# A decoder step on one core: QKV order, per-head statistics, paired heads and the division moved to GpSimd

## The reference, cut to what matters

```python
q = rmsnorm(q, q_gain); k = rmsnorm(k, k_gain)      # per head, over 64 dims
scores = einsum(q, k) * 64 ** -0.5                  # query block against own and previous block of 128
scores = where(valid, scores, -inf)                 # 0 <= qpos - kpos < 128
probs = softmax(concat([scores, sink], -1))[..., :-1]
o = einsum(probs, v) @ w_o
```

## Time and profile before

| | us |
|---|---|
| median of 3 runs | 1272.03 |
| the runs | 1272.03, 1272.52, 1254.83 |
| profiled execution, its own time | 1270.31 |
| profiled execution, span | 1268.5 |
| mean granted TensorE clock | 0.948 of 2.4 GHz |

### The profile page before, as it was taken

The page is one execution under the profiler, slowest core; times in us unless marked ns, Lnnn a source line. Parts: engine busy times, 40 slices in busy tenths (PEclk is TensorE's granted clock), DMA queues, the critical chain, the costliest instruction groups (busy, mean ns, idle before and its releaser), DMA issues.

```text
span 1268.5 us, 25324 instructions
## 1 busy us (share of the span) xinstructions
PE 1199.8 (95%) x9702; PEld 1153.2 (91%) x9710; DVE 726.9 (57%) x1164; ACT 450.4 (36%) x748; POOL 394.5 (31%) x833
## 2 busy tenths in 40 slices
PE   5998799899999999999999777999999999999998
PEld 4985566799999999999998777999999999999998
DVE  6653277467777525776533673454767732676731
ACT  5221245344444213444442123233544411444410
POOL 6046666677878767300003264000000000000000
PEclk9996599999999999999996588999999999999999
DMA  7320200123335333222655232222222322322323
GB/s 245 135 79 25 77 26 26 51 91 120 104 123 178 125 105 109 98 96 98 245 147 134 80 101 79 79 87 96 83 86 99 102 92 73 100 83 99 101 92 103
DMA packets 51206, 129.13 MB, mean 102 GB/s; under 512 B 16940, under 2 KB 20268, under 8 KB 51152
## 3 DMA queue, kind: packets, MB, share of 16 engines
q1 hardware_dynamic: 46880, 115.54, 27.9%
q0 software_dynamic: 4272, 12.89, 2.8%
HBM read 109.91 MB, written 18.21 MB: 101 GB/s over the span
## 4 chain that ended last, share of the span: by engine, by line
PE 86%; DVE 7%; ACT 3%; DMA 2%; issue 2%; SPq 0%; ACTq 0%; DVEq 0%
PE ps L1293 25%; PE ps L1295 25%; PE ps L1294 25%; PE ps L1487 2%; ACT probs L692 2%; PE ps L1337 1%; DVE probs L1052 1%; PE ps L1531 1%; PE ps L1492 1%; DMA x<-in_xT 1%; PE ps L1383 1%; DVE soft L1036 1%; PE ps L1539 1%; DMA rots<-e_scr 1%; PE ps L1452 1%
## 5 line engine op out<-in xcount | busy, mean ns | idle before, releaser
L1293 PE MATMUL ps<-hx_hi,w_hi 128*128 128x260 f32 x1600 | 454.3, 284 | 17.7 <-DVE w_lo L842 11.6
L1295 PE MATMUL ps<-hx_hi,w_lo 128*128 128x260 f32 x1600 | 452.6, 283 | 0.0
L1294 PE MATMUL ps<-hx_lo,w_hi 128*128 128x260 f32 x1600 | 451.2, 282 | 0.0
L590 ACT ACTIVATE w_hi<-w_raw 128x1024 fp32r<-128x1024 f32 (+1 forms) x156 | 175.9, 1127 | 494.7 <-PE ps L1295 494.7
L1293 PEld LDWEIGHTS ps<-hx_hi,w_hi 128*128 128x128 f32 x1600 | 301.6, 189 | 20.2 <-DVE w_lo L842 10.9
L1295 PEld LDWEIGHTS ps<-hx_hi,w_lo 128*128 128x128 f32 x1600 | 301.5, 188 | 0.0
L1294 PEld LDWEIGHTS ps<-hx_lo,w_hi 128*128 128x128 f32 x1600 | 301.4, 188 | 0.1
L842 DVE TENSOR_TENSOR w_lo<-w_raw,w_hi 128x1024 fp32r<-128x1024 f32 (+1 forms) x156 | 205.8, 1320 | 102.4 <-ACT w_hi L590 102.3
L1293 PE MATMUL ps<-hid_hi,w_hi 128*128 128x260 f32 x704 | 199.1, 283 | 0.0
L1294 PE MATMUL ps<-hid_lo,w_hi 128*128 128x260 f32 x704 | 198.7, 282 | 0.0
L1295 PE MATMUL ps<-hid_hi,w_lo 128*128 128x260 f32 x704 | 198.7, 282 | 0.0
(11 more groups left out here) (246 smaller groups left out, 1741.3 us busy)
## 6 DMA issues: line engine op xcount, KB each, us to landing
w_raw<-in_wup SPq DMA_DIRECT2D x88, 512.0 KB, 3.2
w_raw<-in_wdn SPq DMA_DIRECT2D x32, 704.0 KB, 4.0
w_raw<-in_wglu SPq DMA_DIRECT2D x16, 512.0 KB, 3.3
w_raw<-in_wqkv SPq DMA_DIRECT2D x12, 512.0 KB, 3.3
w_raw<-in_wo SPq DMA_DIRECT2D x8, 512.0 KB, 3.4
g_scr<-rec POOLq DMA_DIRECT2D x8, 512.0 KB, 3.0
c_scr<-rec POOLq DMA_DIRECT2D x8, 512.0 KB, 3.0
wst<-g_scr SPq DMA_DIRECT2D x8, 512.0 KB, 8.1
```

The source lines that it names most:

```text
L590: act.activation(w_hi[b][:, 0:kt * P], w_raw[b][:, 0:kt * P], ACT.Copy).then_inc(hi_done, 1)
L1293: pe.matmul(out, wh, xh, start=(k == 0), stop=False)
L1294: pe.matmul(out, wh, xl, start=False, stop=False)
L1295: ins = pe.matmul(out, wl, xh, start=False, stop=(k == kt - 1))
```

## The change

Order and statistics: keys and values are projected first (`qkv_tile`, also in SP's load). Squares, statistics and turns stand among the units. `head_mean` is now a 128x128 block matrix written by VectorE. Keys: its product with the squares gives the mean on all partitions, then square root and reciprocal (`key_rstd`), and `key_norm` writes the output keys and `kp`, the prompt's keys with both gains. Prompt queries are not scaled any more: four matmuls of two columns per tile (`query_stat`) give one value per token on the partition, and its negative inverse times the scale (`nq_rms`) enters the new pass over the scores. The parameter work starts at unit 0 instead of 1 and 2.

Heads: scores and values of two heads alternate between the array's halves. One `tensor_tensor_reduce` per block adds the mask, scales and takes the minimum with the sink, from PSUM into one of six `probs` buffers. ScalarE's exponentials go in place. GpSimd multiplies by the inverse sums. ScalarE copies all seven turned blocks of the even head, VectorE those of the odd. Sample parts stand between pairs. The rest of SP's list, `tables` and all later stages are as before.

```diff
+def qkv_tile(n, b):
+    return 2 * n + b + (8 if isinstance(n, int) and n < 2 else -4)
...
@@ gpsimd
             pool.wait_ge(conv_in, 48)
             pre_rows()
+            for a in range(HEADS):
+                pool.wait_ge(sem("r_done"), a + 1)
+                for blk in range(NB):
+                    v = probs[a % 6][:, blk * 256 + lowest(blk):blk * 256 + 256]
+                    ins = pool.tensor_scalar(v, v, soft_of(a)[2][:, blk:blk + 1], None, ALU.mult)
+                ins.then_inc(sem("p_done"), 1)
             pool.wait_ge(sem("bb_done"), 1)
@@ vector
+            def masked(j, half):
+                dve.wait_ge(sem(f"scored{half}"), j + 1)
+                for e in range(2):
+                    a = 2 * j + e
+                    for blk in (2 * half, 2 * half + 1):
...
+                        ins = dve.tensor_tensor_reduce(
+                            probs[a % 6][:, blk * 256 + lo:blk * 256 + 256],
+                            ps[:, 2 * e + half, c0 + lo:c0 + 256], mask[:, lo:256],
+                            nq_rms[:, n:n + 1], nsink[:, h:h + 1], ALU.add, ALU.min,
+                            soft_of(a)[0][:, blk:blk + 1])
+                    if half:
+                        ins.then_inc(sem("maxed"), 1)
+                    elif e == 1:
+                        ins.then_inc(sem("first_taken"), 1)
+
+            def weights(a):
+                dve.wait_ge(sem("exp_done"), a + 1)
+                _, s, r = soft_of(a)
+                after(tt(s, s, r, ALU.add))
+                dve.reciprocal(r, s).then_inc(sem("r_done"), 1)
...
+            for j in range(NPR):
+                if j + 2 < NPR:
+                    masked(j + 2, 0)
+                attn_turn(2 * j + 1)
+                if j + 1 < NPR:
+                    weights(2 * j + 2)
+                if j in (1, 2):
+                    attn_out(j - 1)
+                if j + 2 < NPR:
+                    masked(j + 2, 1)
...
+                if j >= 3:
+                    attn_out(j - 1)
+                if j + 1 < NPR:
+                    weights(2 * j + 3)
@@ scalar
+            for j in range(NPR):
+                attn_turn(2 * j)
+                if j + 1 < NPR:
+                    attn_exp(2 * j + 2)
...
+                if j >= 1:
+                    attn_out(j - 1)
+                if j + 1 < NPR:
+                    attn_exp(2 * j + 3)
@@ tensor
+            for u in range(12):
+                unit("qkv", u // 2, u % 2, hx_hi, hx_lo, (hx_ready, 0) if u == 0 else None)
+                if u == 0:
+                    pe.wait_ge(ones_in, 16)
+                    norm_stat(0)
+                elif u in (2, 3):
+                    key_stat(u - 2)
+                elif u == 4:
+                    values_turn()
+                elif u >= 5:
+                    query_stat(u - 5)
+                if u in (6, 7):
+                    keys_turn(u - 6)
+                if u == 7:
+                    rows_turn()
+            def scores(j, half):
...
+                for blk in (2 * half, 2 * half + 1):
...
+                    for e in range(2):
+                        r = slice(64 * e, 64 * e + 64)
+                        ins = pe.matmul(ps[:, 2 * e + half, c1 - w:c1],
                                         qkvT[r, (4 * p + g) * TOK + blk * P:(4 * p + g) * TOK + (blk + 1) * P],
+                                        kp[p][r, k0 * P:k0 * P + w], start=True, stop=True)
...
+            for j in range(NPR):
+                turn(2 * j)
+                if j + 2 < NPR:
+                    scores(j + 2, 0)
...
+                turn(2 * j + 1)
+                if j + 2 < NPR:
+                    scores(j + 2, 1)
...
+                pv(j)
```

More of the change, by code:

```diff
@@ L261, in load_unit @@
                     sp.wait_ge(lo_done, u + 1)
-                    src = i[w][bass.ds(row + 2 * n + b, 1)].rearrange("o p c -> (o p) c")
+                    if stage == "qkv":
+                        at = qkv_tile(n, b)
+                    else:
+                        at = row + 2 * n + b
+                    src = i[w][bass.ds(at, 1)].rearrange("o p c -> (o p) c")
                     sp.dma_start(w_raw[b][:, 0:kt * P], src).then_inc(w_in[b], 16)
@@ L677, in _ @@
[L677 to L684, removed]
+                elif u == 3:
+                    for k in range(2):
+                        act.wait_ge(sem("qk_stat"), k + 1)
+                        act.activation(halves(k_rms[k][:]), misc[1 - k], ACT.Sqrt,
+                                       bias=eps[:]).then_inc(sem("k_sd"), 1)
+                elif u >= 4:
+                    tile_square(u, u - 2)
+                    if u == 4:
+                        act.wait_ge(sem("v_turned"), 1)
+                        act.activation(vtok[:].rearrange("p (b c) -> p b c", b=2), ps[:, 6:8, :],
+                                       ACT.Copy).then_inc(sem("vtok_done"), 1)
+                    elif u in (6, 7):
+                        keys_turned(u - 6)
+                    elif u == 9:
+                        query_sd(0)
@@ L1006, in prepare @@
                 elif u == 8:
+                    dve.wait_ge(sem("rows_turned"), 1)
+                    dve.tensor_copy(new_rows[0:NS, :], ps[0:NS, 6, :]).then_inc(sem("new_rows_done"), 1)
                     states()
+                elif u == 10:
+                    query_rstd(0)
+                    dve.memset(soft[:], 0.0)
+                    dve.tensor_scalar(nsink[:], sink[:], -1.0, None, ALU.mult)
+                    after(dve.tensor_scalar(nsink_row[:], sink_row[:], -1.0, None, ALU.mult))
@@ L1019, in _ @@
[L1019 to L1027, removed]
@@ L1043, in attn_norm @@
-            def attn_norm(a):
-                b = a % 2
-                dve.wait_ge(sem("exp_done"), a + 1)
-                s = soft[:, 16 * b:16 * b + 16]
-                after(tt(s[:, 8:12], s[:, 8:12], s[:, 12:16], ALU.add))
-                after(dve.reciprocal(s[:, 12:16], s[:, 8:12]))
-                for blk in range(NB):
-                    lo = P if blk == 0 else 0
-                    v = probs[b][:, blk * 256 + lo:(blk + 1) * 256]
-                    ins = ts(v, v, s[:, 12 + blk:13 + blk], None, ALU.mult)
-                ins.then_inc(sem("p_done"), 1)
@@ new lines, in attn_out, with sample_max @@
+            def attn_out(j):
+                dve.wait_ge(sem("o_hi"), j + 1 if j < 2 else j + 2)
+                tt(tiles(op_lo, j)[:, 0:SEQ], ps[:, out_bank(j), :], tiles(op_hi, j)[:, 0:SEQ].bitcast(F32),
+                   ALU.subtract).then_inc(op_ready, 1)
+            def sample_max():
+                dve.wait_ge(sem("s_turned"), 1)
+                after(dve.tensor_reduce(s_soft[:, 0:1], ps[:, 7, P:2 * P], AX.X, ALU.max))
+                ts(s_soft[:, 1:2], s_soft[:, 0:1], -SCALE, nsink_row[:], ALU.mult,
+                   ALU.min).then_inc(sem("s_maxed"), 1)
@@ new lines, in _ @@
+            NPR = HEADS // 2
+            masked(0, 0)
+            masked(0, 1)
+            query_rstd(1)
+            dve.wait_ge(sem("qn_sd"), 1)
+            after(dve.reciprocal(qn_rms[:], qn_rms[:]))
+            q3 = qkvT[:].rearrange("p (t c) -> p t c", t=12)
+            stt(q_new[:].rearrange("p (t n) -> p t n", t=8), q3[:, 0:8, SEQ:TOK], qk_gain[:, 0:1],
+                qn_rms[:].rearrange("p (t n) -> p t n", t=8), ALU.mult, ALU.mult).then_inc(sem("q_new_done"), 1)
+            weights(0)
@@ L1390, in _, with values_turn @@
-            pe.wait_ge(sem("new_rows_done"), 1)
-            pe.wait_ge(sem("ksT_done"), 1)
+            def values_turn():
+                pe.wait_ge(evac, 6)
+                pe.wait_ge(sem("k_sd"), 1)
+                pe.wait_ge(attn_in, 16 * 13)
+                for blk in range(NB):
+                    for v in range(2):
+                        c0 = (blk % 2) * 256 + v * P
+                        ins = pe.transpose(ps[:, 6 + blk // 2, c0:c0 + P], qt(10 + v, blk * P, P), ident[:])
+                ins.then_inc(sem("v_turned"), 1)
@@ new lines, in rows_turn, with keys_turn @@
+            def rows_turn():
+                pe.wait_ge(sem("qk_normed"), 2)
+                for v in range(4):
+                    ins = pe.transpose(ps[0:NS, 6, v * P:(v + 1) * P], qt((10, 11, 8, 9)[v], SEQ, NS), ident[:])
+                ins.then_inc(sem("rows_turned"), 1)
+            def keys_turn(r):
+                if r == 0:
+                    pe.wait_ge(sem("kc_in"), 16)
+                    pe.wait_ge(sem("k_sd"), 2)
+                else:
+                    pe.wait_ge(sem("ksT_done"), 1)
+                for m in range(8):
+                    c0 = (8 * r + m) * P
+                    ins = pe.transpose(ps[:, 4 + m // 4, (m % 4) * P:(m % 4) * P + P], kc[:, c0:c0 + P], ident[:])
+                ins.then_inc(sem("ks_turned"), 1)
@@ L1392, in _ @@
+            scores(0, 0)
+            scores(0, 1)
+            query_stat(7)
+            pe.wait_ge(sem("qn_sq_done"), 1)
+            pe.wait_ge(sem("q_sd"), 1)
```

(36 more changed lines are left out.)

431 lines of the change are left out of this document (220 added, 211 removed).

## The result

The changed kernel is slower: the ratio to the kernel before is 1.031 (95% interval 1.023 to 1.039), about 40 us. The median of its four runs is 1317.1 us, of the kernel before 1271.8.

The account below looks back on a forecast made before the run. TensorE, busy 95%, was taken to bound the kernel except in the attention, bound by a chain of waits. 1270.3 - 70 (attention) + 93 (late tables) + 2 (slow clock) = 1295.3, say 1296; range 1277 to 1326.

Parts of the forecast that it names:

- part 4: Before dn01: GpSimd's tables start only after the last division, so dn01's weights come late; delay 93 us (80 to 102).
- (a): Rival, attention: granted clock stays at 0.50, TensorE needs 11 us per pair, wo near 200, 1324 us; chance 0.09.
- (b): Rival, attention: VectorE or GpSimd bounds a pair at 9 us, wo at 187, 1310 us; chance 0.10.
- the path to dn01: Sign: TensorE's idle ahead of dn01 leads back over ScalarE's split and the weight load to SP's wait.
- the speed in the stall: Sign, ahead of dn01: missing tables run at 46 us each while VectorE stands still; wrong if they keep 60.
- the length of a pair: Sign, attention: a pair of heads takes 6 to 8 us, with 7.0 taken.
- the idle: Sign: TensorE idles 80 to 100 us ahead of dn01.
- Part 1: QKV stage: statistics and turns among the projection's units add 8.9 us on TensorE; projection ends near 97.1.
- Part 2: Between projection and first turn: evacuation, scores, passes, exponentials, sum, division; first turn about 107, plus 3 us for slow clock.
- Part 3: Attention: eight pairs at 7.0 us, 56 in all; wo starts at 171 instead of 241.4, gain 70 us.
- The rate follows VectorE: Tables on GpSimd: their speed follows how busy VectorE is, 47.4 us each in the attention, 62.8 in up00.
- (c): Rival: tables run at 46 us throughout and are nearly on time, a stall of 8 us, 1208 us; chance 0.06.

Follow-up runs that it names:

- e2: Kernel before, with one added wait so that GpSimd begins the tables only after the last head's division by VectorE; 1371.2 us, ratio 1.086.
- e1: Changed kernel with the division moved from GpSimd back to VectorE; 1227.1 us, ratio 0.970 to the kernel before.
- e5: e1 with SP's wait for the tables also moved behind the loads of dn01's first four units; 1215.4 us, ratio 0.959 to the kernel before.
- e4: Changed kernel with SP's wait for the tables moved behind the loads of dn01's first four units; 1298.4 us, ratio 1.027 to the kernel before.
- e6: e5 with the even head's division on ScalarE, the odd's on VectorE, even head's sum ahead of VectorE's copy; 1209.4 us, ratio 0.955 to kernel before.
- e3: Changed kernel with the next even head's sum and reciprocal ahead of VectorE's copy of the odd head's turned blocks; 1300.2 us, ratio 1.030 to kernel before.
- e7: Changed kernel with GpSimd's division as a product of two tensors, inverse sum broadcast; 1295.8 and 1310.2 us, ratio 1.029 to the kernel before.

## Why the prediction was right

Slower, as forecast: 1296 was predicted, the four runs lie between 1303.0 and 1323.5, their median at 1317.1, inside 1277 to 1326. The mechanism of part 4 is shown from three sides: made alone in the old kernel (e2, +101 us), taken out of the new one (e1, e5), moved in it (e4, e6). The number owes something to a range that reached up to take in rivals (a) and (b): all four runs lie above the forecast, and the profiled execution at 1323.5 also above 1312, the end of the forecast's own range. Of its signs, the path to dn01, the busy GpSimd and the speed in the stall came; the length of a pair (9.4 for 6 to 8), the end of QKV (99.4 for 97), the last store (647.6 for 615) and the idle (102.4 for 80 to 100) missed, and wo at 189.98 stood on the very line of 190 beyond which I had called myself wrong. The sizes:

- **Part 1.** The projection ended near 99.4, not 97.1. Eight records of a query statistic took 0.79 us, 0.10 each, not 0.06: 5.5 us for seven tiles instead of 3.4. Nothing was late for want of VectorE.
- **Part 2.** The first turn came at 114.3, not 107. Of the 7.3 us, 2.3 are the later end of the projection. The first head's division ran from 108.7 to 112.0, 3.3 us instead of 1.8. Then `turn` stood 2.3 us more behind the sample heads' scores in TensorE's list (6.6 us, at a granted clock of 0.50), which I had put into a lump of 3 us elsewhere. The order of that list was there to be read.
- **Part 3 is the step that was mis-sized.** A pair took 9.4 us, not 7.0; the gain was 51.4, not 70, and wo at 190 lies outside my bounds of 160 and 187. Of the 19 us, 7.3 came before the first turn, and the eight pairs with what is between and behind them took 75.7 us where I had 64. The term is the division on GpSimd: 0.90 us per 256 columns, start to start, where I took 0.48 and bounded it by 0.72. The nearest row was of another form, and a bound from another form is none. Rival (b), at 0.10, was nearer than the forecast: it had the engine, 9 us and wo at 187, though at a division of 0.72 and without the ring. With the copy ahead of the sums in VectorE's order, divisions of one pair could not cover the turn and copy of the one before; opening it brought 0.9 us per pair (e3), the cheaper division alone 1.4 (e7), and no run has both, so what is left above 7.0 stays open. VectorE's fused pass, 0.46, was as taken; array halves gave a pair's values in 1.75 against 1.74.
- **Part 4.** Delay 102.5 against 93, just above my bound of 102. Stall rate 45.2 us against 46, the load's 4.0 as taken. The tables took 464 us, not 453. But this is within what they vary by themselves: from the start of wo to dn01 it is 467 us in the changed kernel and e2, and 455 in e3 and e7, a delay of 102.5 to 103 there and 90 here. The forecast of 93 lies between, and whether the two runs at 1303 and 1311 had the shorter one no trace says.
- **The reason given for the tables' speed was too simple.** "The rate follows VectorE", by its busy share, does not hold: in e6 VectorE was busy for 80% and a table took 46.7 us, as in the stall with VectorE idle (45.2), while in up00, at 77%, it took 62 to 69. The share is not it. VectorE's work differs (in the attention most of its passes read from PSUM, in up00 some 80 of its 100 us are passes with two inputs from SBUF), and so does the DMA share (0.15 and 0.40); no run separates these two. The sum used measured rates by stage and so did not need the reason.
- The clock after the hole: 0.50 in 655 to 660, 0.90 in the 6 us behind, 2.1 us in all against the 2 allowed.
- **Rivals.** (a) did not come: the clock rose and fell through the attention, mean 0.81. The argument against it was weaker than it looked, for in the kernel before TensorE was busy for all of 103.6 to 121.0 and the granted clock stayed at 0.50. (c) did not come, and e5 shows what it priced at 1208: 1215.4 with the tables out of the way.

The miss of 19 us in part 3 is the main reason why the forecast lay below all four runs; in the profiled execution the 10 us of part 4 add to it.

By the Trainium skill, "GPSIMD Engine Reference", section 4.1, one-input work runs at roughly line rate on GpSimd. Here the trace does not agree for the form with a scalar per partition, if that counts as one input: by busy time over count it took 3.5 ns per column (43.5 us for 48 instructions of 256 columns), when the product of two inputs, the case which that section calls about twice slower than VectorE, took 2.3 ns (28.1 us for 48).

## What to carry to other kernels

An engine that is idle in a stage may have its slack elsewhere: ask when its list must be finished, by whom it is awaited, and subtract every gain made ahead of that point from the slack. Work with a deadline does not belong behind work that waits for other engines in one ordered list; of the 51 us gained here all was lost, and by the ratio about 40 us more. Put a wait in front of the first instruction that needs it, and look at what else then stands behind it.

## What the runs showed that I had not expected

- GpSimd, 256 fp32 columns in place: 922 ns with a scalar per partition, 613 ns as a product with that scalar broadcast.
- VectorE's fused add, scale, minimum and reduction of 256 columns from PSUM: 0.46 us start to start, with 83 ns to read the accumulator inside it.
- The same table on GpSimd takes 45 us with VectorE idle, 47 in the attention with VectorE busy for 80% (e6), and 54 to 69 beside the work of wo, up00 and dn00; two executions of the same lists can differ by 12 us over three tables.
